# Stick-breaking scores from fp32r high and low parts, in a two-block transformer kernel on one core

## The reference

```python
def stick_breaking(q, k, v):                       # (B, T, 8 * 64), T = 512
    def block_fn(i):
        z = jnp.einsum('bhqd,bhkd->bhqk', qb, k).astype(jnp.float32) * scale
        mask = kpos[None, :] < tq[:, None]
        log_rem = jnp.where(mask, jax.nn.log_sigmoid(-z), 0.0)
        suffix = lax.cumsum(log_rem, axis=3, reverse=True) - log_rem
        a = jnp.where(mask, jnp.exp(jax.nn.log_sigmoid(z) + suffix), 0.0)
        return jnp.einsum('bhqk,bhkd->bhqd', a, v).astype(q.dtype)
```

## Time and profile before

| | |
|---|---|
| median of 3 runs | 1860.25 us (1859.68 to 1860.91) |
| the profiled execution | 1859.73 us, span 1857.9 us |
| PE busy | 1829.4 us, 98% |
| PEld busy | 1631.3 us, 88% |
| DVE busy | 1151.1 us, 62% |
| ACT busy | 769.7 us, 41% |
| POOL busy | 465.7 us, 25% |
| granted TensorE clock | 1.00 |
| chain that ended last | PE 91%, DVE 5%, ACT 2%, issue 1%, DMA 1% |

### The profile page before, as it was taken

One profiled execution on the slowest core, in us unless ns is written; L12 is line 12 of the kernel. 1 busy time (PEld: TensorE's weight loads), 2 busy tenths in 40 slices (PEclk: granted clock), 3 DMA queues, 4 the chain that ended last, 5 costly groups with the idle time before them and its releaser, 6 DMA issues.

```text
span 1857.9 us, 29611 instructions
## 1 busy us (share of the span) xinstructions
PE 1829.4 (98%) x12020; PEld 1631.3 (88%) x12020; DVE 1151.1 (62%) x1677; ACT 769.7 (41%) x1392; POOL 465.7 (25%) x322
## 2 busy tenths in 40 slices
PE   9999999999999999999999999999999999999999
PEld 8999888979988887999988877989767879999887
DVE  7542465555416657899984555646556579999531
ACT  4122455321235644444433324446565544444331
POOL 5433211354341123000034423320003420000343
PEclk9999999999999999999999999999999999999999
DMA  4222100223220012332323233200003213323232
GB/s 166 97 84 89 38 4 21 78 87 98 81 97 7 24 35 93 120 126 94 103 75 102 91 112 123 82 24 1 1 1 114 91 59 122 126 92 103 72 98 102
DMA packets 41048, 145.49 MB, mean 78 GB/s; under 512 B 5072, under 2 KB 5328, under 8 KB 40784
## 3 DMA queue, kind: packets, MB, share of 16 engines
q1 hardware_dynamic: 40912, 143.59, 22.9%
HBM read 140.40 MB, written 2.10 MB: 77 GB/s over the span
## 4 chain that ended last, share of the span: by engine, by line
PE 91%; DVE 5%; ACT 2%; issue 1%; DMA 1%; POOL 0%; SPq 0%; DVEq 0%; ACTq 0%
PE ps L470 23%; PE ps L471 23%; PE ps L472 23%; PE ps L1066 6%; PE ps L1097 5%; PE ps L1082 2%; PE ps L2668 1%; PE ps L2651 1%; DVE xl L560 1%; PE ps L2409 1%; PE ps L2639 1%; PE ps L1276 1%; DVE nm L1143 0%; PE ps L2654 0%; DVE scratch L613 0%
## 5 line engine op out<-in xcount | busy, mean ns | idle before, releaser
L454 POOL TENSOR_TENSOR wl<-raw,wh 128x1024 fp32r<-128x1024 f32 (+1 forms) x170 | 411.1, 2418 | 1021.8 <-ACT wh L446 1021.7
L446 ACT ACTIVATE wh<-raw 128x1024 fp32r<-128x1024 f32 (+1 forms) x178 | 188.9, 1061 | 607.1 <-PE ps L472 541.9
L470 PE MATMUL ps<-xh,wh 128*128 128x264 f32 (+3 forms) x1144 | 384.3, 336 | 6.2 <-ACT wh L446 2.5
L471 PE MATMUL ps<-xl,wh 128*128 128x264 f32 (+3 forms) x1144 | 380.8, 333 | 0.0
L472 PE MATMUL ps<-xh,wl 128*128 128x264 f32 (+3 forms) x1144 | 380.4, 332 | 0.0
L472 PE MATMUL ps<-XSh,wl 128*128 128x256 f32 (+1 forms) x864 | 283.4, 328 | 0.0
L470 PE MATMUL ps<-XSh,wh 128*128 128x256 f32 (+1 forms) x864 | 283.1, 328 | 0.3 <-DVE wl L1749 0.3
L471 PE MATMUL ps<-XSl,wh 128*128 128x256 f32 (+1 forms) x864 | 283.1, 328 | 0.0
L470 PEld LDWEIGHTS ps<-xh,wh 128*128 128x128 f32 x1144 | 215.2, 188 | 33.8 <-issue 7.8
L471 PEld LDWEIGHTS ps<-xl,wh 128*128 128x128 f32 x1144 | 215.3, 188 | 22.5 <-issue 1.0
L472 PEld LDWEIGHTS ps<-xh,wl 128*128 128x128 f32 x1144 | 215.4, 188 | 22.0
(11 more groups left out here) (419 smaller groups left out, 3472.6 us busy)
## 6 DMA issues: line engine op xcount, KB each, us to landing
raw<-wstream SPq DMA_DIRECT2D x176, 512.0 KB, 3.3
rawx<-wpairs SPq DMA_DIRECT2D x44, 512.0 KB, 3.5
raw<-wpairs SPq DMA_DIRECT2D x24, 512.0 KB, 3.5
raw<-wstream SPq DMA_DIRECT2D x10, 528.0 KB, 3.3
h<-xT SPq DMA_DIRECT2D x4, 528.0 KB, 5.8
out<-h SPq DMA_DIRECT2D x8, 256.0 KB, 4.2
xs<-wpairs SPq DMA_DIRECT2D x2, 512.0 KB, 4.5
HF<-wpairs SPq DMA_DIRECT2D x2, 512.0 KB, 5.4
```

Of the source, the lines that this page charges most:

```text
L446: e.activation(wh[p % 2][:, 0:n], raw[c % 2][:, 0:n], ACT.Copy).then_inc(*w_hi(p))
L454: e.tensor_tensor(wl[p % 2][:, 0:n], raw[c % 2][:, 0:n], wh[p % 2][:, 0:n].bitcast(F32), ALU.subtract).then_inc(*w_lo(p))
L470: e.matmul(o, w_h, x_h, start=start, stop=False)
L471: e.matmul(o, w_h, x_l, start=False, stop=False)
```

## The change

The scores become two fp32r products over all 128 rows. For head a, `QS[:, a, :]` holds the high part of its queries in its own 64 rows and the low part in the other 64 rows. The keys of a head are stored twice: their high part in both halves of one tile, their low part in both halves of another. The first product (high keys) adds high times high and high times low, the second (low keys) the two others, so the sum is the full product.

- mix no longer clears `QS`. Queries and keys are scaled into `tmpn` by one VectorE instruction each.
- `break_high_act` on ScalarE copies 64 x 512 high parts: 2 for each of the four query tiles, 4 for each of the four key tiles. `break_low_dve` on VectorE subtracts: 2 for each query tile, 4 for each key tile.
- Heads 0 to 3 have their keys in `KS` and the new `KSL`; heads 4 to 7 in `wh` and `wl`, the weight buffers of ks2 and ks3. So the splits of the first two wout2 tiles move from the end of mix into sb: the first after the output of head 5, the second before the output of head 7.
- The parts of ks3 are made inside nsa: high parts on ScalarE at the start of steps 4 and 6, low parts on VectorE in steps 8 and 10.

```diff
-        QS = sb("QS", [128, 8, T], at=two)
-        KS = sb("KS", [128, 4, T], at=two)
+        QS = sb("QS", [128, 8, T], F32R, at=two)
+        KS = sb("KS", [128, 4, T], F32R, at=two)
+        KSL = sb("KSL", [128, 4, T], F32R, at=two)
...
+                if s in (4, 6) and plan.name == "nsa":
+                    break_high_act(e, on, ("ks", 3), (s // 2 - 2,))
...
+                if s in (8, 10) and plan.name == "nsa":
+                    break_low_dve(e, on, ("ks", 3), (s // 2 - 4,))
...
+        def break_key(a):
+            if a < 4:
+                return KS[:, a, :]
+            return wh[PART["ks", a // 2] % 2][:, T * (a % 2):T * (a % 2) + T]
...
+        def break_high_act(e, on, key, of=(0, 1)):
+            kind, c = key
+            on.wait_ge(*v_out[key])
+            for g in of:
+                p0, p1 = 64 * g, 64 * g + 64
+                src = tmpn[p0:p1, c % 2, 0:T]
+                if kind == "qs":
+                    r = e.activation(QS[p0:p1, 2 * c + g, :], src, ACT.Copy)
+                else:
+                    e.activation(break_key(2 * c + g)[p0:p1], src, ACT.Copy)
+                    r = e.activation(break_key(2 * c + g)[64 - p0:128 - p0], src, ACT.Copy)
+                r.then_inc(*a_out(*key, "high", g))
+        def break_low_dve(e, on, key, of=(0, 1)):
+            kind, c = key
+            for g in of:
+                p0, p1 = 64 * g, 64 * g + 64
+                on.wait_ge(*a_out[key + ("high", g)])
+                src = tmpn[p0:p1, c % 2, 0:T]
+                if kind == "qs":
+                    high, lows = QS[p0:p1, 2 * c + g, :], [QS[64 - p0:128 - p0, 2 * c + g, :]]
+                else:
+                    low = break_key_low(2 * c + g)
+                    high, lows = break_key(2 * c + g)[p0:p1], [low[p0:p1], low[64 - p0:128 - p0]]
+                for dst in lows:
+                    r = e.tensor_tensor(dst, src, high.bitcast(F32), ALU.subtract)
+                r.then_inc(*v_lo(*key, g))
...
+                else:
+                    break_high_act(e, on, key)
...
-            for c in range(4):
+            for c in range(2):
                 split_hi(e, on, PART["ks", c] + 2)
+            for c in range(3):
+                break_high_act(e, on, ("ks", c))
...
-            for k in range(8):
-                a = 64 * (1 - k % 2)
-                e.memset(QS[a:a + 64, k, :], 0.0)
...
+                    if j and MIX[j - 1][0] == "qs":
+                        break_low_dve(e, on, MIX[j - 1])
...
-                    for a in (0, 64):
-                        w = e.scalar_tensor_tensor(QS[a:a + 64, 2 * c + a // 64, :], src[a:a + 64, :], 0.125,
-                                                   r[a:a + 64, :], ALU.mult, ALU.mult)
-                    w.then_inc(*v_out(*key))
+                    e.scalar_tensor_tensor(tmpn[:, c % 2, 0:T], src, 0.125, r, ALU.mult, ALU.mult).then_inc(*v_out(*key))
...
-                e.tensor_tensor(KS[:, c, :], PS[:, 512 * bank["ks", c]:512 * bank["ks", c] + T], rst[:, 0:T],
+                on.wait_ge(*(v_lo["ks", c - 2, 1] if c >= 2 else v_lo["qs", c + 2, 1]))
+                e.tensor_tensor(tmpn[:, c % 2, 0:T], PS[:, 512 * bank["ks", c]:512 * bank["ks", c] + T], rst[:, 0:T],
                                 ALU.mult).then_inc(*v_out("ks", c))
+                if c:
+                    break_low_dve(e, on, ("ks", c - 1))
...
-                e.matmul(ps[:, 0:T - q0], KS[:, a // 2, q0:q0 + 128], QS[:, a, q0:T], start=True, stop=False)
+                on.wait_ge(*a_out["ks", 3, "high", 1])
+                on.wait_ge(*v_lo["ks", 3, 1])
+                e.matmul(ps[:, 0:T - q0], break_key(a)[:, q0:q0 + 128], QS[:, a, q0:T], start=True, stop=False)
+                e.matmul(ps[:, 0:T - q0], break_key_low(a)[:, q0:q0 + 128], QS[:, a, q0:T], start=False, stop=False)
...
+                    if t_ == 3:
+                        on.wait_ge(*score["sb", 7, 0])
+                        split_hi(e, on, PART["wout2", 1])
...
+                    if t_ == 2:
+                        on.wait_ge(*score["sb", 5, 0])
+                        split_hi(e, on, PART["wout2", 0])
...
+                if t_ == 3:
+                    split_lo(e, on, PART["wout2", 0])
+                    split_lo(e, on, PART["wout2", 1])
```

More of the change, by code:

```diff
@@ L2239, in hooks_dve, with break_key_low @@
                     head_low_dve(e, on, key)
+        def break_key(a):
+            if a < 4:
+                return KS[:, a, :]
+            return wh[PART["ks", a // 2] % 2][:, T * (a % 2):T * (a % 2) + T]
+        def break_key_low(a):
+            if a < 4:
+                return KSL[:, a, :]
+            return wl[PART["ks", a // 2] % 2][:, T * (a % 2):T * (a % 2) + T]
+        def break_high_act(e, on, key, of=(0, 1)):
[24 more added lines that the diff above has]
+                r.then_inc(*v_lo(*key, g))
         KEYS_AT = (10, 11, 14)
@@ L2348, in mix_dve @@
                     on.wait_ge(*tile[key])
-                    on.wait_ge(*v_one["zeros"])
-                    for a in (0, 64):
-                        w = e.scalar_tensor_tensor(QS[a:a + 64, 2 * c + a // 64, :], src[a:a + 64, :], 0.125,
-                                                   r[a:a + 64, :], ALU.mult, ALU.mult)
-                    w.then_inc(*v_out(*key))
+                    if c >= 2:
+                        on.wait_ge(*v_lo["qs", c - 2, 1])
+                    e.scalar_tensor_tensor(tmpn[:, c % 2, 0:T], src, 0.125, r, ALU.mult, ALU.mult).then_inc(*v_out(*key))
                 if j in (3, 7):
@@ L2394, in mix_pool @@
             e.memset(Y[1][:, :, 64:66, :], 0.0).then_inc(*p_one("y"))
-            parts_pool(e, on, ("kc", 0), ("ks", 3))
+            parts_pool(e, on, ("kc", 0), ("ks", 1))
         def compress_pe(e, on, t):
@@ L2637, in begin @@
                 ps = claim(on, sb_bank(k), 1, prob["sb", a, j])
-                on.wait_ge(*v_out["ks", 3])
-                e.matmul(ps[:, 0:T - q0], KS[:, a // 2, q0:q0 + 128], QS[:, a, q0:T], start=True, stop=False)
+                on.wait_ge(*a_out["ks", 3, "high", 1])
+                on.wait_ge(*v_lo["ks", 3, 1])
+                e.matmul(ps[:, 0:T - q0], break_key(a)[:, q0:q0 + 128], QS[:, a, q0:T], start=True, stop=False)
+                e.matmul(ps[:, 0:T - q0], break_key_low(a)[:, q0:q0 + 128], QS[:, a, q0:T], start=False, stop=False)
                 on.wait_ge(*a_one["strict"])
```

## The result

| | before | after |
|---|---|---|
| median | 1860.51 us (6 runs, 1859.68 to 1863.24) | 1867.92 us (6 runs, 1864.38 to 1870.32) |
| ratio, 95% interval | | 1.0036 (1.0022 to 1.0049) |
| profiled execution, span | 1859.73, 1857.9 us | 1866.18, 1864.2 us |
| mean granted clock | 1.00 (the profiled run) | 0.991 to 0.994 (all six) |
| PE, DVE, ACT busy | 1829.4, 1151.1, 769.7 us | 1831.6, 1163.9, 784.0 us |

What follows compares the result with a forecast made beforehand. The prediction took TensorE, busy 98% of the span, as the bound. Its terms -3.2 (sb), -0.5 (mix) and +3.1 (nsa) gave -0.6 us, 1859.1 against the profiled 1859.73, stated as 1859.6 for the median; range 1855.4 to 1863.4.

Steps and rivals of the forecast that it cites:

- mix, -0.5: Stage mix: without the eight memsets the product's 0.48 us wait goes and the added parts cost nothing; -0.5 us.
- The scores in sb: Stick-breaking stage: fp32r pairs save 0.88 us per head, 7.0 for eight; after deductions sb is 3.2 us less.
- Head 0's scores: Start of sb: issued while TensorE waits anyway, so their 0.88 us saving brings nothing.
- The weight split, 1.06 + 0.3: sb after head 5's output: the split delays ScalarE's chain 1.06 us, GpSimd's half delays VectorE's RT adds, 0.3 us.
- nsa, +3.1: First block of the sparse stage: added parts on VectorE and ScalarE make TensorE 3.1 us late.
- start dose: Start of nsa: ks2's four low parts on VectorE before the first maximum delay the first transposition; +0.8 us.
- upper bound: nsa: at most all added work counts, 5.6 us of low parts and 2.6 of high parts, 8.2 us.
- the +2.0 for ks3's low parts: nsa, ahead of the maxima of units 10 and 12: 2.79 us of VectorE work, mostly not absorbed; +2.0 us.
- the +0.3 for its high parts: nsa, ahead of unit 4's Exp: two ScalarE copies delay its transposition, partly won back; +0.3 us.
- 1 (absorbed): nsa's first sparse block absorbs the parts, costing only 0.8 us; total -3.6 to -4.3, about 1856; chance 0.23.
- 2 (the queues give nothing back): nsa steps 0 to 12: VectorE's and ScalarE's delays add up, to 8.2 us; total +4.5, 1864.8; chance 0.13.
- 3 (the pair costs what fp32 did): sb: the fp32r pair saves nothing and sb is 1.4 us longer; total +4.0, 1864.2; chance 0.04.

Runs made afterwards that it cites:

- experiment 10: experiment 2 with the first wout2 tile's split moved to sb step 31, GpSimd's half held until VectorE's last add into RT; 1856.82 us, ratio 0.9977.
- experiment 1: The changed kernel plus 25 filler matmuls, results unread, ahead of transpositions of units 0, 3, 4, 10, 11, 12 of nsa's first block; 1862.22 us, ratio 1.0006.
- experiment 7: experiment 5 plus 13 filler matmuls, results unread, ahead of the transpositions of units 0, 3 and 4; 1859.59 us, ratio 0.9990.
- experiment 6: The changed kernel with only ks2's four subtractions moved to steps 56 and 58 of nsa, ks3's parts left at steps 4 to 10; 1865.29 us, ratio 1.0024.
- experiment 5: The changed kernel with ks3's parts moved to nsa's last block, ks2's four subtractions left before the first maximum; 1866.62 us, ratio 1.0033.
- experiment 8: The changed kernel with ks3's parts late and ks2's four subtractions moved behind the maximum of unit 2; 1866.40 us, ratio 1.0017.
- experiment 2: The changed kernel with all twelve part instructions moved from nsa's first block to its last; 1859.02 us, ratio 0.9992.

## Why the prediction was wrong, step by step

**mix, -0.5: right.** The product with `Y`, at 1083.98 in after, no longer waits (0.48 us before), and the parts on VectorE and ScalarE show nowhere on TensorE. Up to nsa 0.58 us are won.

**The scores in sb: right.** The pair and mask of 512 columns are 0.23, 0.24 and 0.06 us in the chain (0.53 forecast, 0.92 before with its mask). Chain of after, behind head 1:

```profile
1357.12 0.70 DVE SPb L2774
...
1357.86 1.12 PE ps L2702 x2
...
1359.63 0.23 PE ps L2689
1359.87 0.24 PE ps L2690
1360.10 0.06 PE ps L2692
```

The five pieces of ScalarE and VectorE that answer to the earlier trace rows are unchanged, and TensorE waits 0.76 us behind them (forecast 0.75). From one head's values' product to the next I had 0.88 us less where no output copy intervenes and 0.39 where one does. The starts of heads 0 and 1 in after and then before (head 2's are 1360.56 and 1353.55):

```profile
1344.91 2.37 PE L2719 MATMUL ps<-Ab,VSB 128*128 128x512 f32 x8
1352.24 2.37 PE L2719 MATMUL ps<-Ab,VSB 128*128 128x512 f32 x8
```

```profile
1336.62 2.37 PE L2668 MATMUL ps<-Ab,VSB 128*128 128x512 f32 x8
1344.84 2.37 PE L2668 MATMUL ps<-Ab,VSB 128*128 128x512 f32 x8
```

7.33 against 8.22 and 8.32 against 8.71: 0.89 and 0.39. Head 0's scores brought nothing, as said: the wait at the start grew from 0.63 to 1.31 us.

**The weight split, 1.06 + 0.3: right in the sum, the second part for another reason than I gave.** From the values of head 5 to those of head 6 after takes 9.61 us (1383.77 to 1393.38) and experiment 10 8.17 (1376.18 to 1384.35): 1.44 against my 1.36. TensorE waits 1.71 us for the softplus there (1.8 forecast), 0.95 more than after heads 1 and 3; the other 0.49 is lost behind that, up to head 6's values. I had only the adds with two SBUF operands stand behind GpSimd's split. What waits is the copy into `RT`, with one; the add behind it takes 0.41 us as ever:

```profile
1388.74 2.36 POOL L455 TENSOR_TENSOR wl<-raw,wh 128x1024 fp32r<-128x1024 f32 x1
...
1390.20 0.99 DVE L2788 COPY RT<-SPb 128x128 f32<-128x128 f32 x1
1390.34 1.12 PE L2702 MATMUL ps<-SPb,cst 128*128 128x512 f32 x2 [1.71 <-DVE SPb L2774]
```

It takes 0.99 us, and 0.23 three us earlier in the same trace; it ends at 1391.19, the split at 1391.10. The Trainium skill, "SBUF — State Buffer", in its box on GpSimd's DMAs, counts such a copy, fp32 from SBUF to SBUF, among the operations that use the shared pair of ports; the trace agrees. sb as a whole brought 2.66 us of 3.2. The missing 0.5 (0.7 with the terms unrounded) is not one term: the stretch up to head 0's values (9.32 against 10.02 us) and the one from head 2's to head 3's (7.54 against 8.22) each gain 0.2 us less than 0.88, and what follows head 5's values another 0.3 less than forecast. I didn't follow these up.

**nsa, +3.1: the step that failed.** Its terms for the work hold. The first transposition stands 0.84 us later (0.8 forecast), and nsa is 3.5 us longer than before in experiment 1, where the clock stays up (fillers included; 3.1 forecast). The forecast named the transposition of unit 12, 3 us later against the end of mix. That transposition is the 13th of the stage; before, in experiment 1, and in experiment 7:

```profile
1237.16 0.33 PE L1082 MATMUL ps<-identR,Pb 128*128 128x128 f32 x1
...
1242.45 0.33 PE L1087 MATMUL ps<-identR,Pb 128*128 128x128 f32 x1 [0.18 <-ACT Pb L1129]
...
1237.45 0.33 PE L1087 MATMUL ps<-identR,Pb 128*128 128x128 f32 x1
```

From the first score on that is 14.39, 17.92 and 15.36 us, and 16.94 in experiment 6 (the row at 1238.52 above), and in all four the clock stood at 1.00 up to there. So all doses cost 3.53 us, the start dose 0.97 (fillers included) and ks3's parts 2.55 (2.3 forecast), and they add up (0.97 + 2.55) as the walk had it. In after the same distance is 21.52 us, 7.13 more than before, and VectorE's waits have not gone, as was forecast, but grown.

What the step left out is the clock. It priced a wait of TensorE at its own length. Here it costs 6 to 8 us more: 7.7 by experiments 5 and 7, 6.1 by after and experiment 1, about 7.5 between the two kinds of runs in experiment 8. In after 3.5 + 6.1 is the 9.6 that nsa lost. The upper bound, "all that is added: 8.2 us", was no bound either: nsa lost 9.57. It bounded the queues, while at 0.50 TensorE's own work is what grows.

With the clock down the doses don't add up. Then VectorE and ScalarE wait for TensorE (4.29 us ahead of the maximum of unit 10), and the +2.0 for ks3's low parts and the +0.3 for its high parts have room: the start dose alone costs 9.0 us, all three 9.6.

The prediction read the granted clock of before, 1.00 in the block, as a fact of the stage. It was a property of that order of work, and not a firm one (one execution in 28 at 0.994). TensorE's longest wait in the block of before is as long as the one that opens experiment 5's fall:

```profile
1248.02 0.41 PE L2509 MATMUL ps<-identR,scratch 128*128 128x128 f32 x2 [0.66 <-DVE scratch L2561]
```

The clock stayed at 1.00 behind this one, and behind another 0.47 us of waiting at 1248.91. So the rows of before couldn't tell that the new wait would be answered with a fall, which argues for a rival and not for a term. The Trainium skill, "TensorE: Matmul & The Clock Gate" (the part on the gate), says that the clock follows how busy the array has been and has two levels; the traces agree, 0.50 and 1.00. The prediction gave it no rival. With the price that only the experiments show, 6 to 8 us, such a rival would have stood at 1865.6 to 1867.6; the profiled run took 1866.18 us, the median is 1867.92.

**The rivals.** 1 (absorbed) is refuted where it stood, by the 3.53 us of experiment 1; the absorption it hoped for exists in the last block, +0.28 us (experiment 2). 2 (the queues give nothing back), with 1864.8, lies nearest to the time, for another reason: its mechanism is refuted by experiments 1 and 7. 3 (the pair costs what fp32 did) is refuted by the chain.

**What stays open.** Why single runs of after take up to 1870.32 us. Their mean clock is lower still (0.991), so the clock fell once more somewhere, as it did in sb in the profiled runs of experiments 5 and 6, but no profile shows such a run of after. Those falls in sb have something in common that the forecast had as harmless. In experiments 5 and 6 the clock falls behind the wait for the first softplus, 0.63 us before and 1.3 now; in the profiled runs of experiments 1 and 8 it falls behind the wait after head 5, 1.71 us with the moved split. Each time it is down for only some 3 us, and sb is 68.0 to 68.2 us instead of 66.65, about 1.4 more. In the profiled run of after the same waits left it up. (The profiled run of experiment 10 has one more such fall, from about 1326 us, at the end of nsa.) That these falls make up the slower runs of after is not shown.

## What to carry to other kernels

A delay put on an engine that feeds TensorE is priced twice: by the wait that it opens, and by what the granted clock may do after it, for which the windows of clock, not the busy share, have to be read. The same instructions can come out either way, so it takes many runs, each with its clock, and not one profile. Small extra work of VectorE or ScalarE belongs where TensorE's units are wide enough to cover it (here the last block, +0.3 us against +9.6 in the first), and where such a wait can't be avoided, matmuls whose result nobody reads can be worth more in it than they cost. A GpSimd split that is moved delays VectorE at its new place: look at every VectorE instruction under it, copies too.

## What the runs showed of the hardware

- A wait of 0.67 us in dense TensorE work was followed by 20 us at a granted clock of 0.50, with TensorE 100% busy (experiment 5); 13 added matmuls of 256 columns removed the fall and 7.7 us (experiment 7).
- Waits of 0.66 us (before, 1248.02) and 0.81 us in other places left the clock at 1.00, one of 1.51 was followed by some 3 us at 0.50 only (experiment 6). Twelve runs of one program fell into two kinds, four at a mean clock of 0.999 and eight at 0.993 to 0.995, 7.5 us apart (experiment 8).
- At 0.50 a pair of 128-column fp32r products takes 0.67 us in place of 0.42.
- A VectorE copy with one SBUF operand, 128x128, took 0.99 and 1.30 us beside GpSimd's split, ending with it, and 0.23 without it. Four subtractions of 64x512 took 4.87 us beside one and 2.79 without.
